# Weight loads of the gated feed-forward groups queued in another order, and the residual's turning and its copies moved

## The reference

```
x = x + y @ w_out[l]
h = rms_norm(x, ffn_norm_w[l])
x = x + (jax.nn.silu(h @ w_gate[l]) * (h @ w_up[l])) @ w_down[l]
...
return rms_norm(x, final_norm_w)
```

## The kernel before

| steps | product | source of the tile |
|---|---|---|
| 0, 1 | `G_M11` | `x_part`, loaded |
| 2, 3 | `G_M12` | `raw`, loaded |
| 4, 5 | `G_M22` | `y_part`, loaded |
| 6, 7 | `G_M21` | `x_part` after an adding DMA from POOL's queue (L887) |
| 8, 9 | `G_SUM` | `x_part` after DVE added `y_part` to it (`sum_weights`, L1558) |
| 10, 11 | `G_LAST` | `w_part`, loaded, and after an adding DMA |
| 12, 13 | `G_ALL` | `x_part` after a third adding DMA |

## Time and profile before

### The profile page before, as it was taken

How to read it: one execution, slowest core, us unless ns; L and a number is a source line. 1 busy time by engine, 2 the same in 40 slices (tenths; PEclk the granted TensorE clock), 3 DMA queues, 4 the chain that set the end, 5 groups by cost and what they waited for, 6 DMA issues and landing times.

```text
span 1221.0 us, 15940 instructions
## 1 busy us (share of the span) xinstructions
PE 1187.2 (97%) x5791; PEld 958.3 (78%) x5791; DVE 837.4 (69%) x1273; ACT 618.9 (51%) x992; POOL 138.3 (11%) x245
## 2 busy tenths in 40 slices
PE   9999999999999999999999999999995999999998
PEld 7876648888888888888888788788874788887886
DVE  6787886786667663336677666546792777688796
ACT  6354455655555553335585254444552455556564
POOL 0000000011011100000002814300010111110320
PEclk9999999999999999999999999999998899999999
DMA  7233321567867843331322211112559587777991
GB/s 246 87 108 103 105 54 51 191 104 207 206 144 167 242 104 97 93 104 55 118 86 70 87 36 53 29 59 70 184 92 208 103 211 202 176 169 272 192 183 69
DMA packets 61966, 156.80 MB, mean 128 GB/s; under 512 B 22466, under 2 KB 22722, under 8 KB 61634
## 3 DMA queue, kind: packets, MB, share of 16 engines
q1 hardware_dynamic: 48882, 111.44, 28.4%
q0 software_dynamic: 12096, 43.00, 20.2%
q10 hardware_dynamic: 912, 1.35, 0.5%
HBM read 147.22 MB, written 2.10 MB: 122 GB/s over the span
## 4 chain that ended last, share of the span: by engine, by line
PE 84%; DVE 6%; ACT 4%; DMA 3%; issue 2%; SPq 2%; ACTq 0%; DVEq 0%
PE PS L2243 81%; DMA x_part<-w_glu 2%; SPq L815 2%; PE PS L2539 1%; DVE wring L1551 1%; ACT wring L1016 1%; DMA raw<-w_stream 1%; PE PS L2319 1%; DVE cacc L1919 0%; DVE hbuf L1580 0%; ACTq L1255 0%; DMA raw<-w_glu 0%; DVE turned L1610 0%; PE PS L2623 0%; DVE wring L1774 0%
## 5 line engine op out<-in xcount | busy, mean ns | idle before, releaser
L2243 PE MATMUL PS<-HH,wring 128*128 128x512 f32 x1176 | 288.7, 397 | 0.9 <-DVE vd L2171 0.9
L2243 PE MATMUL PS<-wring,HH 128*128 128x512 f32 x1152 | 269.7, 393 | 17.5 <-DVE glu_s L1583 16.3
L2243 PEld LDWEIGHTS PS<-wring,HH 128*128 128x128 f32 x1152 | 217.8, 190 | 63.9 <-DVE glu_s L1583 16.7
L2243 PEld LDWEIGHTS PS<-HH,wring 128*128 128x128 f32 x1176 | 215.0, 188 | 44.0 <-issue 1.3
L1551 DVE TENSOR_TENSOR wring<-x_part,wring 128x1024 fp32r<-128x1024 f32 x80 | 97.9, 1223 | 81.1 <-ACT wring L1016 81.1
L1774 DVE TENSOR_TENSOR wring<-raw,wring 128x1024 fp32r<-128x1024 f32 x91 | 112.0, 1232 | 46.1 <-ACT wring L964 46.0
L964 ACT ACTIVATE wring<-raw 128x1024 fp32r<-128x1024 f32 x91 | 95.7, 1056 | 94.2 <-PE PS L2243 66.8
L1016 ACT ACTIVATE wring<-x_part 128x1024 fp32r<-128x1024 f32 x80 | 84.6, 1060 | 110.5 <-PE PS L2243 48.2
L2243 PE MATMUL PS<-AS,wring 128*128 128x512 f32 x528 | 120.4, 389 | 0.0
L2243 PE MATMUL PS<-wring,left_minus 128*128 128x512 f32 x480 | 113.8, 393 | 1.6 <-DVE glu_q L1569 1.6
L2243 PEld LDWEIGHTS PS<-AS,wring 128*128 128x128 f32 x528 | 99.0, 188 | 20.4
(11 more groups left out here) (365 smaller groups left out, 1681.4 us busy)
## 6 DMA issues: line engine op xcount, KB each, us to landing
raw<-w_stream SPq DMA_DIRECT2D x91, 512.0 KB, 3.5
x_part<-w_glu POOLq DMA_DIRECT2D x40, 512.0 KB, 6.3
x_part<-w_glu SPq DMA_DIRECT2D x20, 512.0 KB, 4.7
raw<-w_glu SPq DMA_DIRECT2D x20, 512.0 KB, 6.1
y_part<-w_glu SPq DMA_DIRECT2D x20, 512.0 KB, 8.4
w_part<-w_glu SPq DMA_DIRECT2D x20, 512.0 KB, 13.9
w_part<-w_glu POOLq DMA_DIRECT2D x20, 512.0 KB, 7.6
kept<-w_last POOLq DMA_DIRECT2D x15, 512.0 KB, 7.6
```

The lines of the kernel that those rows point to most:

```text
L2243: return nc.tensor.matmul(out, lhsT, rhs, start=start, stop=stop, skip_group_check=adds)
```

## The change

Four things are changed.

1. `load_group` issues `raw`, `y_part`, `w_part` of group `j` and then `x_part` of the same group. So in the queue the next group's `x_part` stands behind its `raw`, `y_part` and `w_part` instead of ahead of them.
2. The 16 `residual_blocks` move from behind the first group's loads to group 2's: eight behind `raw`, eight behind `y_part`.
3. `turn_residual` moves from behind steps 4 to 7 of group 0 to behind steps 10 (two), 12 (three) and 13 (three).
4. In `last_product` the low parts of pieces 4 and 5 are made ahead of `halves` 9 and 10.

```diff
+        def load_raw(l, j):
+
             for p in range(2):
                 t = glu_tile(l, j, G_M12, p)
...
+        def load_group(l, j):
+
+            if j == 0:
+                load_part(l, x_part, 0, j, 0, 0)
+            load_raw(l, j)
+            if l and j == 2:
+                for m in range(8):
+                    residual_blocks(m)
             load_part(l, y_part, 2, j, 1, 1)
+            if l and j == 2:
+                for m in range(8, 16):
+                    residual_blocks(m)
             load_part(l, w_part, 4, j, 1, 0)
-            if j + 1 < GROUPED:
-                load_part(l, x_part, 0, j + 1, 0, 0)
+            if j:
+                load_part(l, x_part, 0, j, 0, 0)
...
             load_group(1, j)
-            if j == 0:
-                for m in range(16):
-                    residual_blocks(m)
...
-            elif l and 4 <= step < 8:
-                for n in (2 * step - 8, 2 * step - 7):
+            elif l and step in (10, 12, 13):
+                for n in {10: (0, 1), 12: (2, 3, 4), 13: (5, 6, 7)}[step]:
                     turn_residual(n)
...
                 if g == 4:
+                    left_low(P_12, 4)
+                    left_low(P_12, 5)
                     halves(9)
                     halves(10)
-                    left_low(P_12, 4)
-                    left_low(P_12, 5)
```

More of the change, by code:

```diff
@@ L770, in load_part, with residual_blocks @@
                 sp.dma_start(place[:, p], glu_d[l, j, kh, u][:, p * TILE:(p + 1) * TILE]).then_inc(part_loaded[n], 16)
-        def load_group(l, j):
-            if j == 0:
-                load_part(l, x_part, 0, j, 0, 0)
+        def residual_blocks(m):
+            a, b = m // 4, m % 4
+            if m == 0:
+                sp.wait_ge(sem("resid_turned"), KD)
+                sp.wait_ge(feed_sq, KD * FINAL)
+                sp.wait_ge(h_ready, KD * FINAL)
+                sp.wait_ge(sem("lhs_scaled"), 2 * KD)
+            to = resid[32 * b:32 * b + 32].rearrange("p t u (n x c) -> p (t u n) x c", x=4, c=32)
+            from_ = turned[32 * a:32 * a + 32].rearrange("p t n (x c) -> p (t n) x c", c=32)
+            sp.dma_start(to[:, :, a], from_[:, :, b]).then_inc(sem("resid_loaded"), 16)
+        def load_raw(l, j):
             for p in range(2):
@@ L803, in _ @@
                 sp.dma_start(raw[:, j % RAW], src).then_inc(raw_loaded[j % RAW], 16)
[L805 to L815, removed]
         for t in range(loop_end * RING, T_GLU[1]):
```

## The result

The changed kernel takes 1204.81 us (median; 1203.08 to 1205.61), the one before in the same series 1220.26 us. The ratio is 0.9869, 95% interval 0.9852 to 0.9886. So it is faster by 1.3%, but 6.5 us slower than the 1198.3 us forecast, and 1.8 us outside the range. The profiled execution took 1205.61 us with a span of 1203.8.

The account below looks back on a forecast made before the run. PE sets the time, so only its waits and the clock lost by them can be won. Terms: -19.5 - 1.7 - 1.4 - 1.2 + 1.7 = -22.1 us, from median 1220.42 to 1198.3 us; range 1196.2 to 1203.0.

Parts of the forecast that it names:

- The copies in group 1: Second layer: copies ahead of group 2's w_part and x_part make x_part land 1.7 us late; bounds 0 and 5.4.
- a hole of 3.4: Group 1's DMA work: of an add's 6.1 us some 3.4 move nothing; one such hole makes 39.4 into 42.8.
- The upper bound of that wait: x_part of group 2 late by 5.4 us, with a group's recorded DMA share, 30.8 us, in place of 27.1.
- the copies overrun the DMA engines: Rival: group 1 ends 5.4 us late, 1202.0, or 1205.0 with 3.0 us of clock loss; chance 0.14.
- The adds against the copies: Group 1, second layer: adds expected to win against copies; two among them had landed in 5.7 us, 6.1 alone.
- a sign of being wrong: At a group's end: adds landing after more than 8.4 us would show the forecast wrong.
- Boundary 0 to 1: Transposes moved to steps 10, 12 and 13 of group 0: cost taken as 0, bounds 0 and 2.0 us.
- The loads in the other groups: x_part loaded last: its second half lands 1.1 us faster, removing gate_first waits of 1.4 us; bounds 0 and 1.4.
- The small terms: Group 0's wait for q goes, gain 1.7 us; low parts at piece 4 of the down projection, gain 1.2 us.

Follow-up runs that it names:

- four parts: The changed kernel with the sixteen copies in four parts of four, behind x_part of group 1 and raw, y_part and x_part of group 2: 1198.14 us.
- light: Three variants of the changed kernel: transposes two behind step 10, one behind 12, five behind 13, and copies split further: 1197.92, 1197.57 and 1197.36 us.
- four light parts: The changed kernel with copies in four parts of four and transposes two behind step 10, one behind step 12, five behind step 13: 1197.92 us.

## Why the prediction was wrong

**Right in kind.** The wait for `up_second` is gone, with the low clock behind it; so are those for `q`, `gate_first` in the other groups, and `place_even`. The new wait is where it was expected, for `gate_first` at boundary 1 to 2 with ACT waiting for `x_part`. The runs without copies, with long runs, with `x_part` first and with four parts all move it the way that the work of the DMA engines says.

**Where the gain is**, from group start to group start of the two profiled executions, with the forecast behind it: ahead of the second layer's groups 1.56 us (1.1), group 0 1.19 (1.7), group 1 14.30 (17.8), group 2 -2.05 (0), group 3 0.46 (0.3), the rest 1.74 (1.2). That is 17.2 against 22.1, and groups 1 and 2 alone lack 5.6.

**The step that failed is the size of "The copies in group 1": 1.7 us were taken, 7.1 measured** (5.05 of wait and 2.05 of clock in group 2). Its own terms, against the stretch from the landing of `x_part` at 920.7 to that at 965.8:

```profile
920.70:965.80 45.10, 42.93 (x197) 35.03 (x195) 28.07 (x33) 21.07 (x26) 5.14 (x6) 1.00 0.96 210
```

- The time at hand was put at 41.1 us. PE could have gone on at 964.49, and from the landing to PE's start it is 3.7 us (965.8 to 969.54), so the load was due at 960.8: 40.1 us. The 1.1 us by which the earlier `x_part` was to land sooner were not there. One microsecond.
- The work was put at 39.4 us with a hole of 3.4. Here 0.96 x 45.10 = 43.3 us were busy, and the rest 1.8. Together that is 45.1 against 42.8: 2.3 us. The bytes are those that were counted (210 GB/s for 45.1 us are 9.5 MB, and 14 times 0.524 and 16 times 0.131 are 9.4), so the prices were wrong. It was not the copies' price: without them group 1 was busy for 0.76 x 40.04 = 30.4 us, so they added 12.9, and 12.3 had been taken. The loads and adds were too cheap, 27.1 us worked out against these 30.4, and the earlier trace rows already had 30.8 for a group. Why they take more together than each rate says stays open.
- 1.7 + 1.0 + 2.3 = 5.0 us. The upper bound of that wait was 5.4 and held; I chose the low one for the reason that full engines had set the rates, which was wrong.
- SP itself did not arrive in time either: 14 us for each eight copies instead of 9.7, and `x_part` issued 5.4 us after its place was free. That is at most a part of the wait: the engines were full meanwhile, with all copies at the start SP issued `x_part` on time and PE still waited 3.28 us, and `x_part` ahead of `w_part` gained 3.1 us where SP's part would have given 1.2.
- The clock. The forecast had no loss of it, and the rival "the copies overrun the DMA engines" had: 5.4 us of wait and 3.0 of clock, 1205.0 us, given with the overrun's 0.14 and then cut off by a range that ended at 1203.0. This rival is what happened. That its 1205.0 is only 0.2 us from the median is partly luck: it had 8.4 us for wait and clock where 7.1 were measured, and it had nothing for the 0.86 us at boundary 0 to 1. Idle stretch and the one behind it in the changed kernel, as in the earlier trace rows:

```profile
964.49:969.54 5.05, 0.00 (x1) 0.00 (x1) 3.68 (x5) 3.68 (x4) 1.82 (x3) 0.76 0.27 67
969.54:978.00 8.46, 8.46 (x28) 6.81 (x29) 7.07 (x9) 3.30 (x5) 1.68 (x2) 0.74 1.00 197
```

PE worked at the upper level (2.4 GHz) until it idled at 964.49. Behind it a granted share of 0.74 over 8.46 us loses 2.2 us, near the 2.05 by which group 2 is longer. The Trainium skill ("TensorE: Matmul & The Clock Gate", "HAM oscillation") says that waits for DMA bring the slow clock back; this trace agrees with its number.

**The adds against the copies**: I expected the adds to win, as two adds among the copies had landed in 5.7 us. With plain loads under way as well they don't. The two of `x_part` issued in the middle of group 1 (windows 941.5:942 and 945.3:945.8) landed late:

```profile
x_part<-w_glu POOLq DMA_DIRECT2D x1, 512.0 KB, 8.1
...
x_part<-w_glu POOLq DMA_DIRECT2D x1, 512.0 KB, 8.5
```

In the first layer the like took 6.3 and 6.4 us. The later one held ACT for 0.77 us, but not PE. It was above the 8.4 that the prediction had named as a sign of being wrong, in this group alone.

**Boundary 0 to 1**: taken as 0, measured 0.86 us. The low part of step 13 began at 914.36, some 0.6 us late by its transposes (0.9 was said), and the second half of `x_part` then took 5.1 us, not 4.1. It was meant to be spared a load behind it, but `w_part` and its own first half were under way ahead of it. The other runs show how the two add up, by the time from the end of the low part of step 13 to ACT's start on the second half:

| transposes | low part to ACT's start, us | wait of PE, us |
|---|---|---|
| as in the change | 4.3, 4.4, 4.6, 4.7, 4.7, 4.8, 5.0, here 5.2 | 0, 0, 0.31, 0.37, 0.41, 0.48, 0.69, 0.86 |
| light | 5.0, 5.1, 5.4 | 0, 0.23, 0.55 |

So the wait is what the load takes above 4.3 us, or above 4.9 with the light transposes: these do save their 0.6 us. Why the load takes anything from 4.3 to 5.4 us stays open.

**The loads in the other groups**: the right gain for too large a reason. I took 1.1 us of faster landing, from a row of 4.1 that I read as a half with nothing behind it. It is the first half, and the second half and `raw` were issued before it had landed, 2.7 and 3.1 us behind it. In the first layer the second half now lands in 4.9 us instead of 5.2. That was just enough for waits of 0.36.

**The small terms** hold: `q` 1.6 and `place_even` 1.2, each by undoing it.

**Ahead of the second layer's groups** the changed kernel is 1.56 us earlier than before. It had been 3.06 us earlier at the last of the first layer's boundaries: 1.58 from the groups, and 1.48 already at their start, where nothing was changed. In this execution the clock fell once more in the mixer of the second layer; a window of the changed kernel there has a granted clock of 0.59:

```profile
782.00:786.00 4.00, 4.00 (x24) 3.93 (x23) 0.87 (x3) 0.87 (x2) 0.00 (x0) 0.59 0.00 0
```

Of the other profiled executions only that with all copies at the start has it (0.79 from 780 to 785 us). These two start the second layer's groups at 885.2 and 885.5 us, the others with the new order of loads at 883.2 to 884.4, so it costs some 1.5 us when it comes. Nothing in the mixer was changed, and nine kernels with the same order of loads don't have it, so I take it for chance; no run tests that.

## What to carry to other kernels

Work that leaves a queue's critical place still has to be done somewhere: before moving DMAs into a stretch, add up what that stretch's engines must carry until the next load that is waited for, with the busy share as recorded for such a stretch (30.8 us here) and not with rates taken one by one (27.1). If that comes as near to the time at hand as here, split the DMAs and put parts where the next deadline is farthest, here right behind the load that everyone waits for. Order a queue's loads by when their places come free, and price a possible wait of several microseconds together with the clock it may take along.

## What the runs showed of the hardware

- Short DMA pieces are dear. Eight copies of 128 KB in 128-byte runs kept SP for 14 us; the same bytes in 4 KB runs for 5.3 and 8.0 us. Sixteen kept it for 19.4 us in the kernel before, beside two adds, and for 26.2 beside four and the start of a fifth. During the first 14 us in the changed kernel (927.7 to 942) SP's queue had 51.9% of the engines' time and POOL's adds 46.8%, so neither queue stood still.
- A DMA is slowed by what is issued right behind it in its own queue: the second half of `x_part` landed after 7.1 us with 2 MB behind it, and after 4.4 us at the same boundary with nothing behind it.
- What a wait of PE costs in clock, by the group behind it: waits of 2.00 and 2.25 us left it at 1.00 (groups of 40.04 and 40.20 us); waits of 3.28, 4.44, 5.05 and 5.52 us went with 0.96, 0.93, 0.95 and 0.94 (41.41, 42.80, 42.08 and 42.38 us). The loss is 1.4 to 2.8 us, and over these four it does not simply grow with the wait.
- Executions of one kernel differ by 3 to 5 us here: 1198.17 to 1203.15 with `x_part` first, 1197.95 to 1203.20 with all copies at the start, 1197.30 to 1200.72 with four light parts, which hardly wait. The fastest have a mean clock of 0.999 to 1.00, the slowest 0.996 or 0.997. The traces show two places where it falls, behind the wait and in the mixer; which of them made the executions without a trace slow is not shown.
